# A second PSUM bank for the context's gates and states in the feed-forward stage of a two-block kernel

## The chip, the cores and the metric

The kernel runs on one core of one Trainium2 chip. The metric is the device time of one execution in microseconds (us). Before the change three runs took 1398.24, 1388.03 and 1389.52 us, with a median of 1389.52 us.

## The reference, cut to what matters

One token sequence (256 tokens, width 1024) passes two blocks. The first is attention with a SwiGLU feed-forward network. The second mixes tokens with gated linear attention (GLA) and retention, whose starting states come from a context of 256 tokens, and ends in 16 experts that each pick their tokens. The change touches only the context's part:

```python
def _gla_final_state(k, v, log_a):
    b = jnp.cumsum(log_a, axis=1)
    w = jnp.exp(b[:, -1:] - b)
    return jnp.einsum('bthk,bthv->bhkv', k * w, v)

# in _project, for the normalised context hc
pre = einsum('btdr,drk->btdk', gz.reshape(B, T, 2, 16), gla_gate_w) + gla_gate_b
log_a = log_sigmoid(pre) / 16            # two directions, 4 heads of 64
```

The steps for the context are: project it to keys and values; `z` = 32 gate columns; `pre` = the gates before the sigmoid, for two tiles of 128 tokens; the log-sigmoid; the sums over later tokens (a matmul with a triangular matrix) and their exponential, `kw`; keys times `kw`; and the states `sg`, for two directions d and two pairs of heads r. The retention's keys and values are projected after that, and the retention's states `sr` come last.

## The kernel before, in words

Each engine has a program of its own, written as Python generators (lanes), and semaphores between them. In the feed-forward stage a fixed string of turns, the same for all engines, advances three lanes: `g` is the gate-and-up projection of the first block (22 slots of weights), `c` is the context (22 turns) and `f` is a piece of the modulation vectors, on DVE alone. The string is `gfcf` repeated, and after the `f` are used up `gc`. So on PE the order is slot n of `g`, then turn n of `c`, without exception; what waits at the head of a program's queue holds all behind it.

A slot of `g` is 4 blocks of 128 rows of the contraction by 512 columns, for two token tiles, in three matmuls each (L633, L634, L635, from the rounded high part and the low part): 24 matmuls. Two slots make a group. For slot n, ACT rounds the weights to a high part (`top_half`, L2328) and DVE subtracts it (`low`, L1434), both two turns ahead. At the end of a group ACT takes a tanh out of PSUM (L2521), DVE makes two products per tile (L1311) into `GN`, and in the next even turn PE transposes them (`gated_T`, L555) into bank 4, which ACT copies out (L2511). The groups use banks 0 to 3.

The context has banks 5, 6 and 7. Its turns on PE are: 1 to 5 the norm, 6 to 8 the projection `proj(0..2)` into bank 5 (token tile 0) and bank 6 (token tile 1); turn 9 is `z` (L942), in bank 7; turn 10 is `pre` (L950), both token tiles in bank 7, with DVE's addition of the bias (L1868) between them; turns 11 and 12 are `kw` (L962, L964), banks 5 and 6, for d = 0 and 1; turns 13 and 14 are `sg` (L974), where the two states of a direction both go to bank 7, and DVE copies each out (L1883, L1884) before the next may be written; turns 15 to 18 are `proj(3..6)` (L932), banks 5 and 6; then `sr` (L993). In turn 10 DVE goes on to the log-sigmoid: `abs` (L1311), exponential and logarithm on ACT (L2527, L2529), `min` and subtract (L1311), scale (L1871). The last is what PE's turn 11 waits for (`v ctx L`).

DVE's order in a turn n of `g` is: `low(n + 2)`, in turns 6, 8, 10 and 12 a `down_piece` (L1420, L1422), and for odd n the products of the group; its turn of `c` comes behind all that. Weights come in 1 MB pieces on SP's queue, in one order, into 8 places of a ring; each transfer is issued (L2821) when the earlier content of its place has been used.

Of the kernel before, what the change touches and what calls it, by code (L numbers as in the profile page):

```python
# [9 lines left out]
ALU = mybir.AluOpType  # L10
# [160 lines left out]
class Book:  # L171
# [11 lines left out]
    def sig(self, name, *index):  # L183
        engine, lane, *event = name.split()
        key = f"{engine}_{lane}"
        if key not in self.sems:
            self.sems[key] = self.make(f"s_{key}")
        n = self.count[key] = self.count.get(key, 0) + 1
        if event:
            if self.dry:  # L190
                assert (name, *index) not in self.value, (name, index)
                self.value[(name, *index)] = n
            assert self.value[(name, *index)] == n, (name, index)
        self.latest[engine] = (self.sems[key], n)
        return self.sems[key], 1

    def at(self, name, *index):
        if self.dry:
            return None, 0
        engine, lane, _ = name.split()  # L200
        return self.sems[f"{engine}_{lane}"], self.value[(name, *index)]
# [42 lines left out]
def build(nc, D, out, coff):  # L244

    ctx = ExitStack()
    with ctx:
# [7 lines left out]
        sig, at, prev = book.sig, book.at, book.prev  # L255
# [13 lines left out]
        PS = ctx.enter_context(nc.psum_tensor("PS", [128, 8, 512], F32))  # L269
# [54 lines left out]
        SG, SR = arena[:, ARENA - 1536:ARENA - 1024], arena[:, ARENA - 1024:ARENA]  # L324
# [5 lines left out]
        hc, CX, pc, GZc, rl_, ul, stc, GAc = al(2048), al(2048), al(2048), al(256), al(8), al(8), al(4), al(16)  # L330
        assert top[0] <= ARENA - 1536
        hcv, CXv = hc.rearrange("p (k t) -> p k t", k=8), two(CX)
        pcv, pcr = two(pc[:, 0:1600]), two(pc)
# [53 lines left out]
        GWc, GBrc = PR("wuk"), PR("wuv")  # L387
# [60 lines left out]
        for k in FFN:  # L448
            if k == "g" and seen["g"] < len(PLAN["gu"]):
                want_dense("gu", seen["g"])  # L450
            if k == "c" and seen["c"] in (6, 7, 8, 15, 16, 17, 18):
                i = (6, 7, 8, 15, 16, 17, 18).index(seen["c"])
# [96 lines left out]
        def tensor(e):  # L549
            w = Waits(e)  # L550
            mm = e.matmul
# [362 lines left out]
            def context():  # L914
                yield
                yield from norm("nc", pc, (5, 6, 7), lambda k: [at("v nc h", k - 6) if (k - 6) % 4 else at("a nc h", k - 6)] if k >= 6 else [at("a gate row", 0), at("a nf h", 6)])

                def proj(n):
                    g, k0, kk = PLAN_CTX[n]
                    wc = G_CTX[g][1]  # L920
                    s = slot("ctx", n)
                    w.wait_ge(*s.ready)
                    if n == 0:
                        w.wait_ge(*at("a nc h", 4))
                        w.wait_ge(*at("v nc h", 6))
                    for t in range(2):
                        if k0 == 0 and g:
                            w.wait_ge(*(at("v ctx ev", g - 1) if t else at("a ctx ev", g - 1)))
                        if n == 3:
                            w.wait_ge(*at("a ctx kw", 1, t))  # L930
                        for k in range(k0, k0 + kk):
                            i = mm(PS[:, 5 + t, 0:wc], hcv[:, k, 128 * t:128 * t + 128], s.view[:, (k - k0) * wc:(k - k0 + 1) * wc], start=k == 0, stop=k == 7)  # L932
                        if t == 0 and k0 + kk == 8:
                            i.then_inc(*sig("pe ctx t0", g))
                    i.then_inc(*sig("pe ctx slot", n))

                for n in range(3):
                    proj(n)
                    yield
                w.wait_ge(*loaded("par"))  # L940
                for k in range(8):
                    i = mm(PS[0:32, 7, 0:256], GZW[:, k, :], hcv[:, k, :], start=k == 0, stop=k == 7)  # L942
                i.then_inc(*sig("pe ctx z"))
                yield
                w.wait_ge(*loaded("gw"))
                w.wait_ge(*at("v ctx z"))
                for t in range(2):
                    if t:
                        w.wait_ge(*at("v ctx pre", 0))
                    mm(PS[:, 7, :], GZc[0:32, 128 * t:128 * t + 128], GWc[0:32, :], start=True, stop=True).then_inc(*sig("pe ctx pre", t))  # L950
                yield
                L, KW = two(CX[:, 0:1024]), CX[:, 1024:2048].rearrange("p (d t n) -> p d t n", d=2, t=2)
                for d in range(2):
                    for t in range(2):
                        w.wait_ge(*at("v ctx L"))
                        b = 5 + t
                        w.wait_ge(*at("v ctx ev", 1))
                        w.wait_ge(*at("a ctx ev", 1))
                        if d:
                            w.wait_ge(*at("a ctx kw", 0, t))  # L960
                        far = d == t
                        i = mm(PS[:, b, 0:256], C("gt") if d == 0 else C("lt"), L[:, t, 256 * d:256 * d + 256], start=True, stop=not far)  # L962
                        if far:
                            i = mm(PS[:, b, 0:256], C("ones"), L[:, 1 - t, 256 * d:256 * d + 256], start=False, stop=True)  # L964
                        i.then_inc(*sig("pe ctx kw", d, t))
                    yield
                for d in range(2):
                    for r in range(2):
                        w.wait_ge(*at("v ctx kw", d, 1))
                        w.wait_ge(*at("v ctx pre", 1))  # L970
                        if (d, r) != (0, 0):
                            w.wait_ge(*at("v ctx sg", d - 1 + r, 1 - r))
                        for t in range(2):
                            i = mm(PS[:, 7, 0:256], KW[:, d, t, 128 * r:128 * r + 128], pcv[:, t, 256 + 256 * r:512 + 256 * r], start=t == 0, stop=t == 1)  # L974
                        i.then_inc(*sig("pe ctx sg", d, r))
                    yield
                for n in range(3, 7):
                    proj(n)
                    yield
                yield  # L980
                RK = CX.rearrange("p (t d n) -> p t d n", t=2, d=2)
                for h in range(4):
                    w.wait_ge(*at("v ctx rk"))
                    w.wait_ge(*at("v ctx ev", 3))
                    w.wait_ge(*at("a ctx ev", 3))
                    b = 7 if h % 2 else 5
                    if h > 1:
                        w.wait_ge(*at("a ctx sr" if h % 2 else "v ctx sr", h - 2))
                    else:
                        w.wait_ge(*at("v ctx sg", 1, 1))  # L990
                    for d in range(2):
                        for t in range(2):
                            i = mm(PS[:, b, 128 * d:128 * d + 128], RK[:, t, d, 128 * h:128 * h + 128], pcr[:, t, 512 + 128 * h:640 + 128 * h], start=t == 0, stop=t == 1)  # L993
                    i.then_inc(*sig("pe ctx sr", h))
                    if h % 2:
                        yield
# [206 lines left out]
            for t in range(2):  # L1203
                i = tr(PS[0:16, 2, 128 * t:128 * t + 128], AFv[:, t, :])
            i.then_inc(*sig("pe rt at"))
            w.wait_ge(*at("v rt top"))
            for t in range(2):
                i = tr(PS[:, 3, 16 * t:16 * t + 16], AT[0:16, 128 * t:128 * t + 128])
# [37 lines left out]
            for k in range(4):  # L1246
# [4 lines left out]
                for t in range(2):  # L1251
                    i = tr(PS[:, b, 256 * (k % 2) + 128 * t:256 * (k % 2) + 128 * t + 128], SLG[:, 512 * t + 128 * k:512 * t + 128 * k + 128])
# [5 lines left out]
            for grp in range(4):  # L1258
                for x, (f0, fw) in enumerate(THIRD):
# [12 lines left out]
                    for c in range(nch):  # L1272
                        cc = f0 // 128 + c
                        i = tr(PS[:, 4, 128 * c:128 * c + 128], HE[:, 128 * cc:128 * cc + 128])
# [11 lines left out]
                for c in range(NDOWN):  # L1286
# [6 lines left out]
                    for hh in range(2):  # L1293
                        for ee in range(4):
                            o = 1024 * ee + 512 * hh
                            i = mm(PS[32 * ee:32 * ee + 32, 6 + hh, :], HT[:, 128 * c + 32 * ee:128 * c + 32 * ee + 32], s.view[:, o:o + 512],  # L1296
                                   start=c == 0, stop=c == 10, tile_position=(0, 32 * ee))
# [8 lines left out]
        def vector(e):  # L1306
            w = Waits(e)
            tt, ts, cp = e.tensor_tensor, e.tensor_scalar, e.tensor_copy
# [534 lines left out]
            def context():  # L1843
# [21 lines left out]
                L, KW = two(CX[:, 0:1024]), CX[:, 1024:2048].rearrange("p (d t n) -> p d t n", d=2, t=2)  # L1865
                for t in range(2):
                    w.wait_ge(*at("pe ctx pre", t))
                    tt(L[:, t, :], PS[:, 7, :], GBrc, ALU.add).then_inc(*sig("v ctx pre", t))  # L1868
                log_sigmoid("ctxg", CX[:, 0:1024], CX[:, 0:1024], CX[:, 1024:2048]).then_inc(*sig("v ctx"))
                chain()  # L1870
                ts(CX[:, 0:1024], CX[:, 0:1024], 1.0 / 16.0, None, ALU.mult).then_inc(*sig("v ctx L"))  # L1871
# [7 lines left out]
                for d in range(2):  # L1879
                    for r in range(2):  # L1880
                        o = 128 * (2 * d + r)
                        w.wait_ge(*at("pe ctx sg", d, r))
                        cp(SG[0:64, o:o + 128], PS[0:64, 7, 0:128])  # L1883
                        cp(SG[64:128, o:o + 128], PS[64:128, 7, 128:256]).then_inc(*sig("v ctx sg", d, r))  # L1884
                    yield
                GAv = GAc.rearrange("p (t d h) -> p t d h", t=2, d=2)
                w.wait_ge(*at("v ctx lg"))
# [1064 lines left out]
```

## Time and profile before

| | before |
|---|---|
| median of 3 runs | 1389.52 us (1388.03 to 1398.24) |
| profiled execution, its own time | 1398.37 us |
| span in the profile | 1396.4 us |
| PE busy | 1013.8 us, 73% |
| DVE, ACT busy | 529.5 us, 289.3 us |
| mean granted TensorE clock | 0.859 |
| chain that ended last | PE 41%, DMA 39%, DVE 14%, ACT 4% |

The span is cut in three: up to about 713 us the two mixers and the dense feed-forward network, where PE is the busiest engine, then the experts, where the transfer of their weights runs at some 430 GB/s. The context's turns 10 to 14 lie between 366 and 418 us. A time in a row is the start of an instruction from the start of the span; the figure in brackets at a row's end is how long its engine was idle before it, and which instruction of which engine ended that.

### The profile page before, as it was taken

The page shows a single profiled execution, that of the slowest core. Times are in us where ns is not written, and L with a number is a line of the kernel's source. Part 1 is how long each engine was busy: PE and PEld are TensorE (multiplying, and loading weights), DVE is VectorE, ACT ScalarE, POOL GpSimd, SP SyncE. Part 2 cuts the span into 40 slices and gives each one's busy share as a digit, 9 for nine tenths or more (in the row PEclk, how much of TensorE's full clock was granted, in tenths as well). Part 3 has the DMA queues.
Part 4 walks back from the last instruction along what each step waited for, and adds up shares of the span by engine and source line. Part 5 has one row for each costly group of instructions (what it writes and reads, how often), then busy time and mean ns, then how long its engine had stood idle before and what let it go on. Part 6 is the DMA issues. An engine that isn't in the chain of part 4 may idle for free.

```text
span 1396.4 us, 12873 instructions
## 1 busy us (share of the span) xinstructions
PE 1013.8 (73%) x5366; PEld 582.4 (42%) x5366; DVE 529.5 (38%) x983; ACT 289.3 (21%) x457; POOL 28.7 (2%) x42
## 2 busy tenths in 40 slices
PE   1787888799879998899986855665555555555674
PEld 0676767686566786677764211111100111111120
DVE  6976666775543498577665100000000000000002
ACT  3322343552331333551321000000000000000000
POOL 0010000100000001000000000000000000000000
PEclk9997789999999999899996988667877877778687
DMA  9895211576434468232266999999999999999994
GB/s 390 321 369 224 91 65 59 218 284 268 174 118 151 151 248 337 76 129 103 102 251 272 421 429 431 430 432 430 430 429 432 430 429 431 430 432 430 429 432 182
DMA packets 41001, 415.13 MB, mean 297 GB/s; under 512 B 4912, under 2 KB 4912, under 8 KB 7792
## 3 DMA queue, kind: packets, MB, share of 16 engines
q1 hardware_dynamic: 38160, 405.75, 71.1%
q10 hardware_dynamic: 2784, 8.57, 1.7%
q8 instruction: 42, 0.69, 0.2%
q14 instruction: 15, 0.12, 0.0%
HBM read 413.26 MB, written 1.05 MB: 297 GB/s over the span
## 4 chain that ended last, share of the span: by engine, by line
PE 41%; DMA 39%; DVE 14%; ACT 4%; issue 2%; POOL 1%; DVEq 0%; POOLq 0%; ACTq 0%
DMA ring<-in_w_egu 12%; DMA ring<-in_w_ed 10%; DMA arena<-in_w_ed 7%; DMA arena<-in_w_egu 7%; PE PS L633 7%; PE PS L634 7%; PE PS L635 7%; PE PS L1234 4%; PE PS L932 3%; DVE ringR L1434 3%; PE PS L555 2%; PE PS L1296 2%; DVE arena L1311 2%; DMA ring<-in_w_in 1%; ACT ringR L2328 1%
## 5 line engine op out<-in xcount | busy, mean ns | idle before, releaser
L1234 PE MATMUL PS<-ring,arena 128*32 128x512 f32 (+1 forms) x1152 | 173.6, 738 | 107.7 <-DMA ring<-in_w_egu 107.7
L633 PE MATMUL PS<-ringR,arenaR 128*128 128x512 f32 (+1 forms) x520 | 217.4, 418 | 31.6 <-DVE arenaR L1422 24.1
L634 PE MATMUL PS<-ringR,arenaR 128*128 128x512 f32 (+1 forms) x520 | 209.8, 403 | 0.0
L635 PE MATMUL PS<-ringR,arenaR 128*128 128x512 f32 (+1 forms) x520 | 209.4, 403 | 0.0
L1434 DVE TENSOR_TENSOR ringR<-ring,ringR 128x2048 fp32r<-128x2048 f32 (+1 forms) x66 | 148.7, 2255 | 108.9 <-ACT ringR L2328 103.9
L1311 DVE SCALAR_TENSOR_TENSOR arena<-arena,PS 128x256 f32<-128x256 f32 (+2 forms) x68 | 33.3, 498 | 376.3 <-ACT arena L2745 366.5
L2328 ACT ACTIVATE ringR<-ring 128x2048 fp32r<-128x2048 f32 (+1 forms) x66 | 123.8, 1884 | 90.9 <-PE PS L635 61.5
L1234 PEld LDWEIGHTS PS<-ring,arena 128*32 128x32 f32 x1152 | 36.2, 129 | 235.4 <-DMA ring<-in_w_egu 171.2
L1296 PE MATMUL PS<-ring,arena 128*32 128x512 f32 x512 | 88.1, 823 | 53.4 <-DMA ring<-in_w_ed 52.8
L633 PEld LDWEIGHTS PS<-ringR,arenaR 128*128 128x128 f32 x520 | 101.2, 195 | 60.0 <-DVE arenaR L1422 31.0
L555 PE MATMUL PS<-CT,arena 128*128 128x128 f32 (+1 forms) x352 | 65.5, 336 | 79.5 <-DVE arena L1311 27.9
L634 PEld LDWEIGHTS PS<-ringR,arenaR 128*128 128x128 f32 x520 | 100.9, 194 | 24.1 <-issue 1.4
L635 PEld LDWEIGHTS PS<-ringR,arenaR 128*128 128x128 f32 x520 | 100.7, 194 | 24.1
L555 PEld LDWEIGHTS PS<-CT,arena 128*128 128x128 f32 (+1 forms) x352 | 51.3, 174 | 108.1 <-DVE arena L1311 44.7
L1353 DVE CUSTOM_DVE_ANT_0 ring<-ring 128x1024 f32<-128x1024 f32 x80 | 94.8, 1220 | 0.2 <-DVE ring L1382 0.2
L2244 DVE COPY arena<-PS 128x512 f32<-128x512 f32 x4 | 2.8, 692 | 212.0 <-PE PS L1296 212.0
L1234 PE MATMUL PS<-arena 128*32 128x512 f32 (+1 forms) x384 | 52.9, 680 | 35.4 <-DMA arena<-in_w_egu 35.3
L2745 ACT ACTIVATE arena<-PS 128x512 f32<-128x512 f32 (+1 forms) x12 | 6.7, 561 | 346.9 <-PE PS L1234 346.9
L1296 PEld LDWEIGHTS PS<-ring,arena 128*32 128x32 f32 x512 | 16.3, 132 | 125.0 <-DMA ring<-in_w_ed 93.0
L932 PE MATMUL PS<-ring,arena 128*128 128x512 f32 (+1 forms) x128 | 49.3, 539 | 1.5 <-DVE arena L1407 1.5
L1296 PE MATMUL PS<-arena 128*32 128x512 f32 x192 | 32.9, 822 | 23.4 <-DMA arena<-in_w_ed 23.4
L2752 ACT ACTIVATE arena<-PS 128x512 f32<-128x512 f32 x4 | 2.4, 597 | 206.8 <-PE PS L1296 206.8
(328 smaller groups left out, 866.3 us busy)
## 6 DMA issues: line engine op xcount, KB each, us to landing
ring<-in_w_egu SPq DMA_DIRECT2D x48, 2048.0 KB, 35.6
ring<-in_w_ed SPq DMA_DIRECT2D x32, 2048.0 KB, 34.4
ring<-in_w_vad SPq DMA_DIRECT2D x40, 1024.0 KB, 6.9
ring<-in_w_egu SPq DMA_DIRECT2D x24, 1536.0 KB, 30.0
arena<-in_w_egu SPq DMA_DIRECT2D x16, 2048.0 KB, 35.6
arena<-in_w_ed SPq DMA_DIRECT2D x12, 2048.0 KB, 32.5
ring<-in_w_in SPq DMA_DIRECT2D x22, 1024.0 KB, 4.8
ring<-in_w_gu SPq DMA_DIRECT2D x22, 1024.0 KB, 4.8
```

The source lines that it names most:

```text
L555: return e.transpose(o, i, ident[0:k, 0:k])
L633: mm(o, xh(k, t), hi[:, c], start=k == 0, stop=False)
L634: mm(o, xh(k, t), s.viewr[:, c], start=False, stop=False)
L635: i = mm(o, xl(k, t), hi[:, c], start=False, stop=k == nk - 1)
L932: i = mm(PS[:, 5 + t, 0:wc], hcv[:, k, 128 * t:128 * t + 128], s.view[:, (k - k0) * wc:(k - k0 + 1) * wc], start=k == 0, stop=k == 7)
L1234: i = mm(PS[32 * ee:32 * ee + 32, b + a_, 0:fw], XEv[:, k, grp, 32 * ee:32 * ee + 32], wv[:, ee, a_, :], start=k == 0, stop=k == 7, tile_p ...
L1296: i = mm(PS[32 * ee:32 * ee + 32, 6 + hh, :], HT[:, 128 * c + 32 * ee:128 * c + 32 * ee + 32], s.view[:, o:o + 512], start=c == 0, stop=c ...
L1311: return e.scalar_tensor_tensor(out=o, in0=a, scalar=s, in1=b, op0=o0, op1=o1)
L1353: i = e.tensor_tensor_reduce(out=wv, in0=wv, in1=CB[:, 1024 * b:1024 * b + 1024], scale=1.0, scalar=0.0, op0=ALU.mult, op1=ALU.add, accum_ ...
L1434: tt(s.viewr, s.view, high(S, n), ALU.subtract).then_inc(*sig(f"v {S} lo", n))
L2328: act(high(S, n), s.view, ACT.Copy).then_inc(*sig(f"a {S} hi", n))
L2745: act(TA[:, 512 * (n % 2):512 * (n % 2) + fw], PS[:, 2 * (n % 2), 0:fw], ACT.Tanh, scale=0.5).then_inc(*sig("a moe ta", n))
```

## The change

Token tile 1 of `pre` and state r = 1 of `sg` go to bank 6 and no longer to bank 7; DVE reads them there. Bank 6 held the context's projection of token tile 1 and then the `kw` sums of token tile 1. The waits follow: `pre` of token tile 1 waits for DVE's copy of the projection's group 1 (`v ctx ev`, 1) instead of DVE's addition for token tile 0; state r = 1 waits for ACT's exponential of the last `kw` in bank 6 (`a ctx kw`, 1, 1); a state of d = 1 waits for the copy of the state of d = 0 in the same bank, where each state waited for the one just before it. `proj(3)` writes token tile 1 into bank 6 and has a new wait for the copy of the last state (`v ctx sg`, 1, 1). The instructions, their number and their shapes are unchanged.

```diff
@@ tensor, context, proj(n)
                         if n == 3:
                             w.wait_ge(*at("a ctx kw", 1, t))
+                            if t:
+                                w.wait_ge(*at("v ctx sg", 1, 1))
@@ tensor, context, turn 10
                 for t in range(2):
                     if t:
-                        w.wait_ge(*at("v ctx pre", 0))
-                    mm(PS[:, 7, :], GZc[0:32, 128 * t:128 * t + 128], GWc[0:32, :], start=True, stop=True).then_inc(*sig("pe ctx pre", t))
+                        w.wait_ge(*at("v ctx ev", 1))
+                    mm(PS[:, 7 - t, :], GZc[0:32, 128 * t:128 * t + 128], GWc[0:32, :], start=True, stop=True).then_inc(*sig("pe ctx pre", t))
@@ tensor, context, turns 13 and 14
-                        if (d, r) != (0, 0):
-                            w.wait_ge(*at("v ctx sg", d - 1 + r, 1 - r))
+                        if r:
+                            w.wait_ge(*at("a ctx kw", 1, 1))
+                        if d:
+                            w.wait_ge(*at("v ctx sg", 0, r))
                         for t in range(2):
-                            i = mm(PS[:, 7, 0:256], KW[:, d, t, 128 * r:128 * r + 128], pcv[:, t, 256 + 256 * r:512 + 256 * r], start=t == 0, stop=t == 1)
+                            i = mm(PS[:, 7 - r, 0:256], KW[:, d, t, 128 * r:128 * r + 128], pcv[:, t, 256 + 256 * r:512 + 256 * r], start=t == 0, stop=t == 1)
@@ vector, context, turn 10
-                    tt(L[:, t, :], PS[:, 7, :], GBrc, ALU.add).then_inc(*sig("v ctx pre", t))
+                    tt(L[:, t, :], PS[:, 7 - t, :], GBrc, ALU.add).then_inc(*sig("v ctx pre", t))
@@ vector, context, turns 13 and 14
-                        cp(SG[0:64, o:o + 128], PS[0:64, 7, 0:128])
-                        cp(SG[64:128, o:o + 128], PS[64:128, 7, 128:256]).then_inc(*sig("v ctx sg", d, r))
+                        cp(SG[0:64, o:o + 128], PS[0:64, 7 - r, 0:128])
+                        cp(SG[64:128, o:o + 128], PS[64:128, 7 - r, 128:256]).then_inc(*sig("v ctx sg", d, r))
```

## Rows read from the trace of the kernel before

**Rows 1.** The page, part 4: the chain that ended last, by engine.
```profile
PE 41%; DMA 39%; DVE 14%; ACT 4%; issue 2%; POOL 1%; DVEq 0%; POOLq 0%; ACTq 0%
```

**Rows 2.** Stretches: length; busy PE, PEld, DVE, ACT, POOL; PEclk; DMA share, GB/s.
```profile
368.00:373.36 5.36, 0.01 (x1) 0.01 (x1) 4.01 (x4) 1.12 (x1) 0.00 (x0) 0.81 0.41 171
373.36:378.10 4.74, 4.74 (x9) 2.66 (x10) 1.92 (x2) 0.65 (x1) 0.00 (x0) 0.50 0.00 0
...
401.60:405.50 3.90, 3.90 (x10) 3.14 (x11) 0.58 (x2) 0.00 (x0) 0.00 (x0) 0.56 0.00 0
...
415.86:419.30 3.44, 3.44 (x8) 2.74 (x9) 1.29 (x3) 0.00 (x0) 0.00 (x0) 0.52 0.00 0
...
424.00:481.00 57.00, 57.00 (x200) 36.06 (x199) 17.69 (x25) 11.79 (x15) 0.00 (x0) 1.00 0.48 166
...
800.00:1390.00 590.00, 344.61 (x2104) 75.90 (x2104) 21.73 (x30) 16.23 (x29) 1.64 (x2) 0.78 0.98 419
```

**Rows 3.** The timeline around turn 10: start, length, engine, line [idle before <-releaser].
```profile
353.25 2.29 DVE L1434 TENSOR_TENSOR ringR<-ring,ringR 128x2048 fp32r<-128x2048 f32 x1
...
366.62 1.12 PE L950 MATMUL PS<-PT,arena 32*128 32x512 f32 x2
...
369.22 2.29 DVE L1434 TENSOR_TENSOR ringR<-ring,ringR 128x2048 fp32r<-128x2048 f32 x1 [7.17 <-ACT ringR L2328]
...
372.62 0.68 DVE L1868 TENSOR_TENSOR arena<-PS,PT 128x512 f32<-128x512 f32 x1
...
373.36 2.07 PE L950 MATMUL PS<-PT,arena 32*128 32x512 f32 x2 [5.62 <-DVE arena L1868]
...
375.36 0.80 PE L633 MATMUL PS<-ringR,arenaR 128*128 128x512 f32 x1
375.46 0.69 DVE L1868 TENSOR_TENSOR arena<-PS,PT 128x512 f32<-128x512 f32 x1 [2.16 <-PE PS L950]
...
376.19 1.22 DVE L1311 SCALAR_TENSOR_TENSOR arena<-arena 128x1024 f32<-128x1024 f32 x1
...
382.92 0.70 PE L962 MATMUL PS<-arena,CT 128*128 128x256 f32 x2 [0.42 <-DVE arena L1871]
```

**Rows 4.** The timeline from slot 13 to the projection: turns 13 and 14.
```profile
391.46 0.58 PE L633 MATMUL PS<-ringR,arenaR 128*128 128x512 f32 x1
...
397.12 2.28 DVE L1434 TENSOR_TENSOR ringR<-ring,ringR 128x2048 fp32r<-128x2048 f32 x1
397.24 1.03 PE L974 MATMUL PS<-arena 128*128 128x256 f32 x4
...
399.32 1.73 DVE L1311 SCALAR_TENSOR_TENSOR arena<-arena,PS 128x256 f32<-128x256 f32 x4
...
401.25 0.30 DVE L1884 COPY arena<-PS 64x128 f32<-64x128 f32 x1
401.60 1.65 PE L974 MATMUL PS<-arena 128*128 128x256 f32 x4 [3.34 <-DVE arena L1884]
...
409.75 0.60 PE L555 MATMUL PS<-CT,arena 128*128 128x128 f32 x4
...
410.19 1.03 PE L974 MATMUL PS<-arena 128*128 128x256 f32 x4
410.39 0.60 ACT L2511 ACTIVATE arena<-PS 128x512 f32<-128x512 f32 x1 [12.57 <-PE PS L555]
...
412.89 2.29 DVE L1434 TENSOR_TENSOR ringR<-ring,ringR 128x2048 fp32r<-128x2048 f32 x1 [9.00 <-ACT ringR L2328]
...
415.86 2.07 PE L974 MATMUL PS<-arena 128*128 128x256 f32 x4 [4.64 <-DVE arena L1884]
...
423.97 7.03 PE L932 MATMUL PS<-ring,arena 128*128 128x512 f32 x16
```

**Rows 5.** SP's timeline: the first transfer of the experts' weights.
```profile
713.60 1.13 SPq L2821 DMA_DIRECT2D ring<-in_w_egu  x2
```

**Rows 6.** What SP's queue waited for from 520 to 860 us: total, times, longest.
```profile
SPq L2821 <- PE PS L555: 16.3, 1, 16.3
```

## The prediction

> **What bounds the kernel now.** I read the chain of waits first: PE carries 41% of it and the experts' transfers 39% [rows 1]. Then the table of stretches, cut at the places where PE stopped. The context's turns lie in the first half, where PE is the busiest engine; from 424 to 481 us, just behind them, it is busy without a break at full clock, with DMA at a share of 0.48 [rows 2]. From 800 us the transfers fill the span at 0.98 [rows 2], so work saved before counts only if that stream also starts earlier. It does: the first expert weights are asked for at 713.60 us [rows 5], and SP's queue had stood 16.3 us until PE was done with the mixer's last transposes [rows 6]. In between, each piece is issued when the slot before it in the ring is used up. I take a gain at 424 us as a gain at the end, 1 for 1.
>
> Last the timeline of the two places. PE stops three times for a bank: 5.62 us at `pre` [rows 3], 3.34 and 4.64 us at `sg` [rows 4], 13.60 us together. Behind each stop it also runs slow: the granted clock is 0.50 for 4.74 us after the first, 0.56 for 3.90 us after the second, 0.52 for 3.44 us after the third [rows 2]. 0.50 is the lower of TensorE's two levels, 1.2 GHz of 2.4. In each case the engine had idled for some microseconds before.
>
> **Turns 13 and 14 (`sg`).** Before: PE starts the first state at 397.24 and comes to the projection at 423.97 [rows 4], 26.73 us. Work without waits: a state is 2 matmuls of 256 columns, 0.85 us (the fence at 410.19 shows 1.03 us busy with the tail of the pipeline; a projection's matmul, 512 columns, takes 7.03 / 16 = 0.44 us for each of two passes, so 256 columns take 0.43) [rows 4]; four states 3.4 us. A slot takes 397.24 - 391.46 = 5.78 us [rows 4]; slots 14 and 15 take 11.56. The transposes take 410.19 - 409.75 = 0.44 [rows 4]. Sum 15.4 us, so 11.3 less. The other way round: stops 3.34 + 4.64 = 7.98; lost clock 3.90 x 0.44 + 3.44 x 0.48 = 3.37; sum 11.35. I take 11.35.
>
> Does anything else hold PE there? With the change the times are: states 0 and 1 from 397.24, slot 14 from 398.95, transposes at 404.7, states 2 and 3 from 405.2, slot 15 from 406.9, the projection from 412.6. Slot 14's low part was made two turns before; slot 15's ends on DVE at 397.12 + 2.28 = 399.4; the group's products that the transposes want end at 399.32 + 1.73 = 401.05 [rows 4]. The third state waits for the copy of the first, at 401.25 + 0.30 = 401.55, the fourth for that of the second, some 0.6 us later, against 405.2. All come in time. DVE's third copy stood at 415.2 behind the low part of slot 16 (412.89), that behind ACT, which had idled 12.57 us for the transposes at 410.39 [rows 4]: these follow PE, and come 5.0 us earlier with it.
>
> The new wait: `proj(3)` writes token tile 1 to bank 6 at 412.6 + 8 x 0.43 = 416.1. The last copy comes after the transposes at 404.7 by the distance of before, 412.89 + 2.29 - 409.75 = 5.43 us [rows 4] for the low part of slot 16, then two states' copies of about 0.6: 411.3. It costs nothing, with 4.8 us to spare. Queued behind it on PE are the projection's other half, slot 16 and all that follows; ACT's copy of the projection's token tile 0 waits for the same event already.
>
> **Turn 10 (`pre`).** PE would go on at once: token tile 0 at 366.62, token tile 1 at 367.5, slot 11 at 368.3 instead of 375.36 [rows 3]; slot 11's low part is there since 353.25 + 2.29 [rows 3]. It ends at 374.1. But turn 11 waits for the scaled log-sigmoid, at 382.92 [rows 3]. That chain runs on DVE: low part of slot 12 (369.22), rounding of a `down_piece`, addition for token tile 0 (372.62), then for token tile 1 (375.46, now behind PE's 2.16 us), `abs` (376.19) and on [rows 3]. Only the addition moves: back to back it comes 0.61 us after the first (the step between two such DVE instructions; a length of 0.68 overlaps), at 373.23, and the whole chain 375.46 - 373.23 = 2.23 us earlier. So turn 11 starts at 382.92 - 2.23 = 380.69, and PE idles 380.69 - 374.1 = 6.6 us in front of it, in place of 5.62 in front of `pre`. **The stop moves; it does not go.** What is late next is the log-sigmoid.
>
> After it the clock should be low as after the stop before: 4.74 us at 0.50, 2.37 us lost [rows 2]. Before, the loss lay within the log-sigmoid's shadow; now it lies behind it, in `kw` and slot 12. Net: -2.23 + 2.37 = +0.14 us. Bounds: no fall of the clock gives -2.23; the low level lasting as long as it did in all, (1 - 0.81) x 2 x 5.36 = 2.04 within the stop and 4.74 after it, 6.78 us at half, gives -2.23 + 3.39 = +1.16. I take +0.14, since the new stop is nearest in length to that of 5.62 us.
>
> **Nothing else is added.** Instructions and shapes are the same. `pre` for token tile 1 waits for a copy made 14 us before, the second state for ACT's last exponential, some 4 us before it: both free. SP's transfers for slots 17 to 20 and the projection are released by the same slots' ends and move with them, at DMA shares of 0.41 and 0.48 [rows 2].
>
> **Sum.** -11.35 + 0.14 = -11.2 us; by the bounds -13.6 to -10.2. Against the profiled execution's 1398.37 that is 1387.2; its own time is 8.85 above the median, 1389.52, and the edit has nothing to do with that difference. On the median: **1378.3 us**, 0.8% less.
>
> **The rivals.** A measurement of this kernel tells about 1% from no change, 13.9 us.
>
> *The clock stays up at turn 11.* The sum is then -13.6, 1375.9. For: at 397.24 to 401.60 PE idled 3.34 us, and the clock fell only when it had restarted [rows 2, 4]. Against: 6.6 us is longer than each stop after which it fell. Chance 0.12.
>
> *The waits only change their name.* As turn 10's stop goes to turn 11, those of `sg` could go to slot 16 or the transposes, if DVE and ACT were the bound. Then nothing is left of 11.35: 1389.5 + 0.1 = 1389.6. Against: ACT had idled 12.57 us before 410.39 until PE's transposes, and DVE 9.00 us before 412.89 until ACT [rows 4]; neither is the bound. A half-way outcome (one of the two stops) would be 1384. Chance 0.10. The Trainium skill, page TensorE: Matmul & The Clock Gate, section HAM oscillation — how this bites in real kernels, reports that adding PSUM double-buffering to a matmul kernel gave no further gain. By that report the time here would be that of before, 1389.5. The trace disagrees for `sg`, where the copy is what PE waits for, and agrees for turn 10, where the next wait takes its place.
>
> *The last copy comes too late for `proj(3)`.* Slower. Place: bank 6 between the projection's two halves. The copy is last in DVE's turn 14, behind the low part of slot 16, itself behind ACT's copy and rounding. From 416.1 each microsecond of delay costs one; it decides the sign from 416.1 + 11.2 = 427.3, which is 16 us after my 411.3. For: it is the one wait that the change adds on PE, and it closes a ring, since DVE's queue ahead of the copy holds a piece that ACT makes after PE's transposes. If that piece also had to wait for its weights or for a slot in the ring, the copy could be late by tens of us; at 440 the time would be 1389.5 - 11.2 + (440 - 416.1) = 1402. Against: before, DVE began it 2.5 us after ACT's copy began (410.39, 412.89), which leaves no time for a wait on weights [rows 4]. Chance 0.05.
>
> *The change doesn't do what it says:* the second state is held by another wait, that for the exponential in bank 6. It is on DVE's path to the first state anyway for d = 1, and 4 us earlier for d = 0; 1389.5. Chance 0.03.
>
> **How the numbers follow.** Forecast 0.70. The noise of medians (three runs spread over 10 us, two of them within 1.5) takes about 0.13 of it over the line of 1%, and two thirds of the first rival's 0.12 is over it: faster by over 1% 0.21. Slower 0.05. The rest within 1%: 0.74. The range runs from below the first rival's 1375.9 by 3 us of noise, 1373, to 1387, which takes in the half-way outcome and leaves most of the cases without change and the slower one out.
>
> **What would show it.** PE's idle before the second `pre` (5.62) and the two before L974 (3.34, 4.64) are gone. PE idles about 6.6 us before the first L962, ended by L1871, which starts 2.2 us earlier; a granted clock near 0.5 for 4 to 5 us follows it, and nowhere else up to 481 us. So the gain is used up at the end of slot 12, and the first L974 still comes near 397.2. The first L932 of `proj(3)` comes at 412.7 in place of 423.97, its two halves without a gap. The first expert transfer is issued at 702.4 in place of 713.60. Wrong would be: PE idle before L633 of slots 14 to 16, ended by L1434, or before L555, ended by L1311; a gap within `proj(3)`; or 713.60 moving by less than PE gained.

## The result and the profile after

The changed kernel is faster, by less than 1%: median 1386.38 us of 20 runs (1382.94 to 1393.44), against 1397.09 us of 20 runs of the kernel before (1388.03 to 1410.72). The ratio, changed over before, is 0.9929, with a 95% interval of 0.9919 to 0.9938: 0.7% less, known to 0.1%. The profiled execution took 1387.48 us, its span is 1385.5 us, and PE was busy for 1013.7 us, as before.

The chain that ended last after the change, page, part 4, answering to [rows 1]:

```profile
PE 41%; DMA 40%; DVE 13%; ACT 4%; issue 1%; POOL 1%; DVEq 0%; POOLq 0%; ACTq 0%
```

The balance is the same. What changed is seen from turn 10 on. This is the timeline of the changed kernel, where the second gate matmul is no longer a row of its own, answering to [rows 3]:

```profile
365.97 1.98 PE L952 MATMUL PS<-PT,arena 32*128 32x512 f32 x4
...
368.57 2.29 DVE L1438 TENSOR_TENSOR ringR<-ring,ringR 128x2048 fp32r<-128x2048 f32 x1 [7.18 <-ACT ringR L2332]
...
371.97 1.28 DVE L1872 TENSOR_TENSOR arena<-PS,PT 128x512 f32<-128x512 f32 x2
373.29 1.23 DVE L1315 SCALAR_TENSOR_TENSOR arena<-arena 128x1024 f32<-128x1024 f32 x1
...
380.01 1.22 PE L964 MATMUL PS<-arena,CT 128*128 128x256 f32 x2 [6.29 <-DVE arena L1875]
```

The two gate matmuls run together, and the two additions too. The stop of 5.62 us before the second gate matmul is gone, and a stop of 6.29 us stands before the sums, ended by the last instruction of the log-sigmoid.

From the first gate matmul to the first state, 366.62 to 397.24 [rows 3, 4], were 30.62 us. Now turns 13 and 14, answering to [rows 4]:

```profile
396.59 1.89 PE L978 MATMUL PS<-arena 128*128 128x256 f32 x8
...
403.91 0.60 PE L555 MATMUL PS<-CT,arena 128*128 128x128 f32 x4
...
404.35 1.89 PE L978 MATMUL PS<-arena 128*128 128x256 f32 x8
404.55 0.60 ACT L2515 ACTIVATE arena<-PS 128x512 f32<-128x512 f32 x1 [7.38 <-PE PS L555]
...
407.05 2.29 DVE L1438 TENSOR_TENSOR ringR<-ring,ringR 128x2048 fp32r<-128x2048 f32 x1 [5.53 <-ACT ringR L2332]
409.37 0.28 DVE L1887 COPY arena<-PS 64x128 f32<-64x128 f32 x1
409.67 0.30 DVE L1888 COPY arena<-PS 64x128 f32<-64x128 f32 x1
410.00 0.28 DVE L1887 COPY arena<-PS 64x128 f32<-64x128 f32 x1
410.30 0.30 DVE L1888 COPY arena<-PS 64x128 f32<-64x128 f32 x1
...
411.68 7.03 PE L934 MATMUL PS<-ring,arena 128*128 128x512 f32 x16
```

396.59 - 365.97 is again 30.62 us: nothing was gained at the gates. That the two agree to the hundredth is luck; in the five other profiles of the changed kernel or of one half of it the distance lies between 30.34 and 31.08 us. The states come in pairs with no stop, and the projection follows the first state by 15.09 us in place of 26.73. The stretch from the first gate matmul to the projection, which I call the stretch from here on, went from 57.35 us to 45.71, so it is 11.64 us shorter. The last copy was out at 410.60, before the projection had begun, and its 16 matmuls take 7.03 us as before.

The granted clock, as stretches of the changed kernel (columns as in [rows 2]), answering to [rows 2]:

```profile
374.00:380.00 6.00, 0.00 (x0) 0.00 (x0) 2.48 (x4) 5.41 (x5) 0.00 (x0) 0.83 0.50 176
380.00:384.60 4.60, 4.59 (x11) 3.67 (x12) 4.34 (x7) 2.50 (x5) 0.00 (x0) 0.50 0.00 0
...
396.60:411.70 15.10, 15.10 (x70) 12.44 (x69) 9.25 (x15) 4.97 (x5) 0.00 (x0) 1.00 0.40 140
...
800.00:1380.00 580.00, 341.62 (x2072) 75.91 (x2072) 22.51 (x31) 16.97 (x30) 1.69 (x3) 0.78 0.98 418
```

Of three low stretches behind a stop one is left, 4.6 us at 0.50 behind the moved stop; the pairs of states and their slots run at 1.00. SP's first transfer of expert weights answers to [rows 5]:

```profile
702.46 1.64 SPq L2825 DMA_DIRECT2D ring<-in_w_egu  x2
```

It comes 11.14 us earlier than at 713.60, and the span ends 10.9 us earlier. So PE's gain did pass through the stage where the transfers fill the span.

### The profile page after: what moved, and what is told of

The parts are those of the page before. It is cut to its first block, busy times and chain, and to the rows that moved or that the text cites. A ratio compares the mean times of both kernels' runs of the same rounds, so it can differ in the third digit from the quotient of the medians.

```text
span 1385.5 us, 12873 instructions
## 1 busy us (share of the span) xinstructions
PE 1013.7 (73%) x5366; PEld 582.6 (42%) x5366; DVE 529.2 (38%) x983; ACT 289.4 (21%) x457; POOL 28.7 (2%) x42
## 4 chain that ended last, share of the span: by engine, by line
PE 41%; DMA 40%; DVE 13%; ACT 4%; issue 1%; POOL 1%; DVEq 0%; POOLq 0%; ACTq 0%
DMA ring<-in_w_egu 24%; DMA ring<-in_w_ed 12%; PE PS L633 7%; PE PS L634 7%; PE PS L635 7%; PE PS L934 3%; PE PS L1238 3%; DMA arena<-in_w_ed 2%; DVE ringR L1438 2%; PE PS L555 2%; PE PS L1300 2%; DMA ring<-in_w_in 1%; DVE arena L1315 1%; ACT ringR L2332 1%; PE PS L1288 1%
## 5 line engine op out<-in xcount | busy, mean ns | idle before, releaser
L1238 PE MATMUL PS<-arena 128*32 128x512 f32 (+1 forms) x384 | 56.0, 714 | 28.5 <-DMA arena<-in_w_egu 28.4
```

What stands on the lines that cost most here:

```text
L1238: i = mm(PS[32 * ee:32 * ee + 32, b + a_, 0:fw], XEv[:, k, grp, 32 * ee:32 * ee + 32], wv[:, ee, a_, :], start=k == 0, stop=k == 7, tile_p ...
```

## The experiments

Each ran 4 to 12 times, beside 11 to 29 runs of the kernel before on the same chip. Ratios are with 95% intervals. The stretch is read from the one profile of each run. It scatters much less than whole times: kernels with the same work there agree within 0.5 us, since what the clock does elsewhere is not in it.

**The change again**, for scale.

> The changed kernel itself, beside the kernel before on the same chip. Theory A (the two stops at the states and the slow clock behind them are gone, 11.6 us at the projection; the stop at the gates only moves; about 1 us is given back later where the clock is low longer): 10 to 11 us less, ratio 0.992 to 0.993. Rival (most of the difference is one of chips and runs): nearer 5 us.

Measured: 1387.72 us against 1396.09, ratio 0.995 (0.9927 to 0.9972), 8.4 us less: short of the 10 to 11 expected, whose ratio of 0.993 the interval just takes in. The 20 runs (0.9929) and a third measurement below (0.9927) are nearer to theory A. Its profiled execution took 1404.89 us: up to the gates it is 19 us late, at a granted clock of 0.64 from 100 to 200 us where the first two profiles have 0.80. The stretch is 46.17 us there. A single execution can thus be off by more than the change is worth, for reasons that lie ahead of it.

**The gates alone.**

```diff
 # turn 10 as changed (DVE's addition reads the same bank), turns 13 and 14
 # as before; arguments cut
-                        w.wait_ge(*at("v ctx pre", 0))
-                    mm(PS[:, 7, :], GZc[...], GWc[0:32, :], ...)
+                        w.wait_ge(*at("v ctx ev", 1))
+                    mm(PS[:, 7 - t, :], GZc[...], GWc[0:32, :], ...)
```

> Only the gates of token tile 1 go to bank 6; the states stay in bank 7 with their waits. Theory A (the stop moves from the second gate matmul to the sums, which wait for the log-sigmoid, and takes its slow clock along): within 1 us of before; the first state starts where it did, near 397 us. Rival B (the rest of the stop is worth what the log-sigmoid chain gains): 2.2 us less. Rival C (the whole stop is gained): 5.6 to 8 us less.

Measured: 1397.60 us against 1396.09, ratio 1.0021 (1.0003 to 1.0040). PE in its timeline:

```profile
366.09 1.98 PE L950 MATMUL PS<-PT,arena 32*128 32x512 f32 x4
380.13 1.22 PE L962 MATMUL PS<-arena,CT 128*128 128x256 f32 x2 [6.29 <-DVE arena L1871]
...
396.43 1.03 PE L974 MATMUL PS<-arena 128*128 128x256 f32 x4
400.80 1.56 PE L974 MATMUL PS<-arena 128*128 128x256 f32 x4 [3.34 <-DVE arena L1884]
...
415.05 2.07 PE L974 MATMUL PS<-arena 128*128 128x256 f32 x4 [4.64 <-DVE arena L1884]
423.21 7.03 PE L932 MATMUL PS<-ring,arena 128*128 128x512 f32 x16
```

The stretch is 57.12 us, 0.23 less than before. The stop moved, the two others stand. Rivals B and C are out, since no time is gained at all. Theory A said within 1 us; the median is 1.5 us above, and the interval lies just above 1. The stretch shows no such loss, so whatever it is lies outside it, and it is not explained here.

**The states alone**, twice.

```diff
 # turns 13 and 14 as changed, turn 10 as before (on DVE too); arguments cut
-                        w.wait_ge(*at("v ctx ev", 1))
-                    mm(PS[:, 7 - t, :], GZc[...], GWc[0:32, :], ...)
+                        w.wait_ge(*at("v ctx pre", 0))
+                    mm(PS[:, 7, :], GZc[...], GWc[0:32, :], ...)
```

> Only the states r = 1 go to bank 6; the gates stay in bank 7. Theory A: the whole gain of the change, 10 to 11.6 us less; PE idles 5.6 us before the second gate matmul as before. Rivals B and C: 2 to 8 us short of the changed kernel.

Measured: 1383.81 us against 1396.09, ratio 0.9915 (0.9898 to 0.9933), stretch 45.73 us. The stretch says that the gates' part is worth nothing; the time left room for it to cost 1 or 2 us. So both ran once more, side by side.

> The changed kernel once more, beside the one with the states alone. Theory A (the gates' part is worth nothing, and the difference between the two seen so far, ratios of 0.993 and 0.995 against 0.9915, is scatter in the stretches before and behind): both at 0.9925, intervals overlapping. Rival (the gates' part costs 1 to 2 us, by the slow clock behind the sums): this one 1 to 2 us above the other again.

> The states alone in two banks, once more. Theory A: the same time as the changed kernel within 1 us, ratio near 0.9925. Rival: 1 to 2 us below it.

Measured: the change 1385.37 us, ratio 0.9927 (0.9906 to 0.9948); the states alone 1387.33 us, 0.9931 (0.9909 to 0.9952). Stretches 45.69 and 45.71. The order of the two turned round, so no difference between them is shown: what was seen before fits scatter, and the stretches agree within 0.04 us.

**The banks with the old waits.**

```diff
                         if r:
                             w.wait_ge(*at("a ctx kw", 1, 1))
-                        if d:
-                            w.wait_ge(*at("v ctx sg", 0, r))
+                        if (d, r) != (0, 0):
+                            w.wait_ge(*at("v ctx sg", d - 1 + r, 1 - r))
 # and, in turn 10, for t = 1
+                        w.wait_ge(*at("v ctx pre", 0))
```

> The changed kernel's banks with the waits of before added again: the second gate matmul waits for the addition of the first, each state for the copy of the one before it. Theory A (the waits, not the bank that an engine reads, carry the gain): 57.3 us from the first gate matmul to proj(3), as before, and the time of before. Rival (part of the gain is that DVE and PE no longer work in the same bank): a part of the 11.6 us stays, 2 us or more.

Measured: 1398.21 us against 1397.11, ratio 1.0004 (0.9988 to 1.0021), stretch 57.42 us. Nothing is gained by working in two banks as such. Here the second bank pays only in that a wait may go.

**A filled stop.** Twelve further matmuls, whose output nobody reads, stand in the stop before the sums.

```diff
 # tensor, context, ahead of the sums
+                w.wait_ge(*at("v ctx pre", 0))
+                for k in range(12):
+                    mm(PS[:, 7, 0:256], ident, hcv[:, k % 8, :], start=True, stop=True)
```

> The changed kernel with 12 further matmuls of 128x256 on PE ahead of the sums, whose output nobody reads; they fill some 5.1 us of the stop of 6.3 us. Theory A (the lower clock after the stop costs 2.2 us, and follows from PE's idleness): granted clock near 1.0 in the 4 us behind the sums' start, 43.4 us from the first gate matmul to proj(3) in place of 45.7. Rival (the clock's fall has nothing to do with the stop, or the extra matmuls come in the way): 45.7 us or more.

Measured: 1383.64 us against 1397.11, ratio 0.9902 (0.9876 to 0.9928). PE, and the clock in two stretches that cover the stop and what follows:

```profile
370.85 5.34 PE L957 MATMUL PS<-arena,CT 128*128 128x256 f32 x24
377.29 0.70 PE L967 MATMUL PS<-arena,CT 128*128 128x256 f32 x2 [1.10 <-DVE arena L1878]
```
```profile
374.00:380.00 6.00, 4.90 (x23) 3.92 (x22) 4.58 (x5) 5.54 (x8) 0.00 (x0) 1.00 0.19 79
380.00:384.60 4.60, 4.60 (x23) 3.69 (x22) 1.73 (x5) 0.00 (x0) 0.00 (x0) 1.00 0.00 0
```

The sums start 14.04 us after the first gate matmul, in this run (377.29 - 363.25) as in the change's profile (380.01 - 365.97). Behind them the clock stays at 1.00, and the stretch is 43.44 us, 2.27 less than the change's 45.71. That is the price of the low clock behind the stop, by itself: 5 us of useless work ahead of the sums saves it.

**Slot 12 on PE before the sums.**

```diff
 # tensor, context: nothing in turn 11, the sums of d = 0 in turn 12,
 # those of d = 1 at the head of turn 13
+                yield
                 for d in range(2):
                     for t in range(2):
                         w.wait_ge(*at("v ctx L"))
 ...
-                    yield
+                    if d == 0:
+                        yield
```

> The changed kernel, but PE takes slot 12 before the sums of direction 0, and the sums of direction 1 stand with the states of direction 0; the other engines keep their order. Theory A (what is late after the change is only the log-sigmoid, and PE has a slot to do meanwhile): the stop of 6.3 us before the sums and the slow clock of some 2.4 us behind it go, 8 to 9 us less than the changed kernel, some 19 us less than before. Rival (the chain on DVE and ACT behind the sums is the bound by now, low parts of slots 14 and 15): PE waits for low parts there, and under 3 us are gained.

Measured: 1384.14 us against 1396.09, ratio 0.9916 (0.9905 to 0.9927), stretch 43.73 us: 2 us less than the change, not 8 to 9. Theory A was wrong in its number, and the rival named the wrong wait:

```profile
381.45 1.09 PE L555 MATMUL PS<-CT,arena 128*128 128x128 f32 x4 [4.60 <-DVE arena L1317]
```

PE did slot 12 at once and then stood for the transposes of group 5. This is the order in which DVE and ACT came to what these need:

```profile
376.80 0.69 DVE L1877 TENSOR_SCALAR arena<-arena 128x1024 f32<-128x1024 f32 x1
377.42 2.29 DVE L1440 TENSOR_TENSOR ringR<-ring,ringR 128x2048 fp32r<-128x2048 f32 x1
379.63 1.72 DVE L1317 SCALAR_TENSOR_TENSOR arena<-arena,PS 128x256 f32<-128x256 f32 x4
```
```profile
374.45 1.06 ACT L2535 ACTIVATE arena<-arena 128x1024 f32<-128x1024 f32 x1
...
378.63 0.66 ACT L2527 ACTIVATE arena<-PS 128x256 f32<-128x256 f32 x2
```

The products (379.63) are on DVE behind the end of the log-sigmoid (376.80) and a low part, and the tanh that they need (378.63) is on ACT behind the logarithm (374.45). The log-sigmoid holds up not one consumer but two. The clock fell behind this stop too, to 0.50 for the first 2.6 us.

**The log-sigmoid ahead on DVE.**

```diff
 # vector: low("gu", 12) and down_piece(2) out of the slots' turn 10, into
 # log_sigmoid, between abs and the wait for ACT
                 stt(u, x, -1.0, x, ALU.mult, ALU.max).then_inc(*sig(f"v {S} abs"))
+                if S == "ctxg":
+                    low("gu", 12)
+                    down_piece(2)
                 w.wait_ge(*at(f"a {S} ln"))
```

> The changed kernel, but DVE makes the additions of the gates and abs ahead of the low part of slot 12 and the down_piece of that turn, and does these two while ACT makes the exponential and the logarithm. PE's order is that of the changed kernel. From the first gate matmul to the first matmul of proj(3) the changed kernel took 45.7 us. Theory A (the log-sigmoid's chain is all that holds PE after the change): the sums start about 4 us earlier, the stop before them is 2.3 us and not 6.3, and the slow clock of 2.2 us behind it may go too: 39.5 to 41.7 us on this stretch, 4 to 6 us less than the changed kernel. Rival (something else on DVE, the low part of slot 12, becomes late for PE): a stop before L633 of slot 12 and under 2 us gained.

Measured: 1381.27 us against 1397.11, ratio 0.9884 (0.9856 to 0.9912). PE before the sums:

```profile
372.67 0.70 PE L964 MATMUL PS<-arena,CT 128*128 128x256 f32 x2 [1.73 <-DVE arena L1879]
```

The stop is 1.73 us, the clock stays at 1.00, and the stretch is 38.89 us, 6.8 less than the change's. Of these, 4.56 us are the stop (6.29 - 1.73), and the rest is the 2.27 us of low clock that the filled stop measured. The stop shrank by more than the 3.4 us of work moved, because that work had first waited for ACT's rounding, and the additions do not: `abs` starts 2.74 us after the first gate matmul, where it was 7.32. I had not counted this, so the result lies 0.6 us beyond the range I gave.

**Both orders.** The two edits above together.

> Both reorderings on top of the change: slot 12 on PE before the sums of direction 0 (in the run of that alone the stretch from the first gate matmul to proj(3) was 43.7 us, since PE stopped 4.60 us before the transposes of group 5, whose products stood on DVE behind the log-sigmoid), and the log-sigmoid ahead of the low part of slot 12 on DVE. Theory A (the log-sigmoid's chain holds the products too): that stop shrinks to some 0.7 us, the stretch to 38.5 us, 7 us less than the changed kernel, and the clock stays up. Rival (ACT's tables and tanh, not DVE's order, make the products late): the stop before the transposes stays at 3 us or more, 42 us.

Measured: 1375.64 us against 1397.11, ratio 0.9845 (0.9818 to 0.9873), stretch 37.12 us. This is the fastest version of all; by the two ratios it takes about 0.8% less than the change. These are its DVE, and the whole stretch in one row:

```profile
365.85 1.48 DVE L1878 TENSOR_TENSOR arena<-PS,PT 128x512 f32<-128x512 f32 x2 [5.80 <-PE PS L952]
367.37 1.22 DVE L1317 SCALAR_TENSOR_TENSOR arena<-arena 128x1024 f32<-128x1024 f32 x1
368.51 2.29 DVE L1440 TENSOR_TENSOR ringR<-ring,ringR 128x2048 fp32r<-128x2048 f32 x1
370.83 0.43 DVE L1426 CAST arenaR<-arena 128x512 fp32r<-128x512 f32 x1
371.29 0.69 DVE L1428 TENSOR_TENSOR arenaR<-arena,arenaR 128x512 fp32r<-128x512 f32 x1
372.10 1.22 DVE L1317 SCALAR_TENSOR_TENSOR arena<-arena 128x1024 f32<-128x1024 f32 x1
```
```profile
364.60:401.70 37.10, 37.07 (x161) 29.30 (x161) 26.02 (x35) 20.32 (x22) 0.00 (x0) 1.00 0.41 143
```

The rounding work fills the time in which DVE had waited for ACT, the stop before the transposes is gone, and PE is busy for 37.07 of 37.10 us at full clock. Nothing is left to gain on this stretch by waits; only less work on PE would do it.

**Both orders, the gates in one bank.**

```diff
 # both orders; turn 10 on PE and DVE with PS[:, 7, :] and the old wait
-                        w.wait_ge(*at("v ctx ev", 1))
+                        w.wait_ge(*at("v ctx pre", 0))
```

> Both reorderings and the states in two banks, but the gates of both token tiles in bank 7 again, with the old wait. Theory A (the second gate matmul waited long only because the addition stood behind the low part of slot 12 and the down_piece; with the new order on DVE it comes at once): PE idles about 1 us before the second gate matmul, the stretch from the first gate matmul to proj(3) is 38 to 38.5 us (37.12 with the gates in two banks), 19 to 21 us less than before. Rival (the second bank for the gates is needed as soon as the log-sigmoid is early): a stop of 3 us or more before the second gate matmul, with a low clock behind it, 41 us.

Measured: 1376.72 us against 1396.72, ratio 0.9862 (0.9842 to 0.9883), stretch 38.24 us, and this row:

```profile
367.37 1.12 PE L952 MATMUL PS<-PT,arena 32*128 32x512 f32 x2 [0.85 <-DVE arena L1878]
```

The old stop of 5.62 us shrinks to 0.85 by the order on DVE, with one bank. Only with the stop behind it gone does the second bank for the gates gain anything, 38.24 - 37.12 = 1.1 us on the stretch. That is one profile against one; the intervals of the two ratios overlap.

## Why the prediction was right and wrong

**The turns of the states: right, mis-sized by 0.3.** The sum gave 11.35, the projection came 11.64 us earlier against the first state. The slot had been counted at 5.78 us, from a row (391.46) that starts while the matmuls ahead of it, 391.21 to 391.80, still run. In the changed kernel a state pair and a slot take 403.91 - 396.59 = 7.32, so 5.6 for the slot, and two slots make up the 0.3. The states alone give it all, the same banks with the old waits none of it. The margin of `proj(3)` was stated as 4.8 us; the last copy was out 4.5 us before the second half's turn (411.68 + 3.43 - 410.60), so the rival that made the change slower did not occur.

**The gates: right.** The stop moved (6.6 forecast, 6.29 read) and brought its low clock along (4.74 us at 0.50 forecast, 4.60 at 0.50 read); net +0.14 forecast, 0.00 read. That the loss is the clock's was an argument then; the filled stop shows it, 2.27 us. The first rival, a clock that stays up, was wrong for the change; it is what the run with the log-sigmoid ahead shows, where the stop is 1.73 us.

**One to one to the end: right within about 1 us in the profile, open beyond that.** From the projection to the first transfer of expert weights were 289.63 us before and 290.78 after, a loss of 1.15 us that I took for a cost at first. It arises at one place in the second block, shown in the last section, where 13.59 us became 14.82. The changed kernel's three profiles have 14.82, 13.51 and 14.81 there, and the two of the states alone 13.30 and 14.81. So one and the same kernel shows both values, and no profile shows that the change causes the longer one. But the three profiles without the states' gain all have the shorter one, and the interval of the 20 runs is 8.7 to 11.3 us of gain, just under the stretch's 11.64. A loss of some tenths to 3 us behind the stretch is therefore not excluded. In all thirteen profiles the distance to the first transfer lies between 287.8 and 290.8 us. That this transfer came at 702.46, where 702.4 was forecast, is partly luck: the profile after was 0.65 us ahead at the first gate matmul already (366.62, 365.97), and had gained 0.3 more than forecast at the states.

**The time: right value for one execution, wrong level.** The sum against the profiled execution gave 1387.2; the median after is 1386.4. I then moved it down by 8.85 to the median of the three runs shown. Two of those three were low for this kernel: over 20 runs its median is 1397.09, which is 1.3 below the profiled execution. Hence 1378.3 was 8 us too low, and the 1386.4 is within the range of 1373 to 1387 by 0.6 us only. Three runs could not say which of 1398.24 and 1388.03 was the common value; the profile's own time was a fourth, 1398.37, and stood with the upper.

**The chances: wrong, by one step.** The steps added up to -0.8%, and I called that "within 1%", since the prediction held that "a measurement of this kernel tells about 1% from no change". That was the step that failed. No row gave this 1%; the nearest thing was the spread of the three runs, 10 us. 20 runs on each side tell 0.1%, and -0.7% is seven times that away from no change. The mechanism had been read to the microsecond, and both ends of its sum, -10.2 and -13.6, spoke for faster; I let the line of 1% overrule it. So 0.74 went to no difference and only 0.21 to faster, against the sum on the same page.

**The waits that only change their name: right for the gates, wrong for the states.** The Trainium skill, page TensorE: Matmul & The Clock Gate, section HAM oscillation — how this bites in real kernels, reports of one kernel that PSUM double-buffering gave no further gain. Here that is so for the gates (ratio 1.0021) and not for the states (0.9915 and 0.9931). What decides in this kernel is whether the next thing that the engine needs is ready.

## What to carry to other kernels

A second buffer gains the stop only if the next wait on the same queue is already over. So read on in the timeline to the next consumer of the same chain, and then to the one after (here the transposes). When an engine stands for the result of a chain on other engines, look at what lies ahead of the chain in their queues: moving 3.4 us of unhurried work into a gap of the chain gave 6.8 us, where the second bank for the gates had given nothing. Compare kernels over a stretch between two instructions around the change: one profile each agreed there within 0.5 us, while whole times scattered by several. And before you call a forecast no change, ask how many runs will be compared: three runs spread over 10 us here, and 20 told 0.7% clearly.

## What was not expected of the hardware

On this stretch a stop of 1.73 us before the sums left the granted clock at 1.00, and so did the useless matmuls, which left 1.10 us idle; behind stops of 3.34 us and more it fell each time, to between 0.50 and 0.62 over the next 2.6 to 5.2 us. The same stop did not always cost the same. Behind the stop of 6.29 us the changed kernel's stretch took 45.71, 46.17 and 45.69 us in its three profiles. And in the second block PE waits 5.38 us, works 3.7 us at 0.50, and waits 2.6 us again. The second wait and the time behind it, before and then after the change:

```profile
562.40:564.99 2.59, 0.00 (x0) 0.03 (x1) 2.31 (x5) 2.59 (x7) 0.00 (x0) 0.98 0.57 177
564.99:568.40 3.41, 3.41 (x10) 2.69 (x11) 3.24 (x5) 3.41 (x2) 0.00 (x0) 0.64 0.05 19
```
```profile
550.10:552.70 2.60, 0.01 (x1) 0.04 (x1) 2.33 (x5) 2.60 (x7) 0.00 (x0) 0.50 0.54 178
552.70:556.10 3.40, 3.40 (x8) 2.73 (x9) 3.23 (x5) 3.40 (x2) 0.00 (x0) 0.50 0.05 18
```

In the profile of before the clock is back at 0.98 during the second wait and falls again behind it; in that of after it stays at 0.50 throughout. The work is the same. From the transposes between the two waits to the next matmuls behind the slot are 13.59 us in the one (558.70 to 572.29) and 14.82 in the other (546.41 to 561.23), and as said above either value comes up in profiles of the same changed kernel.
